# Token-major gates and outputs of three mixers with 512-column weight operands, the merged sum turned back, and the last norm spread over three engines

## What is computed

```python
def second_block(x, mem, ...):
    h = rmsnorm_2(x, norm_mix[l])
    (hq, hi, hff, hfb, hg, nq, nk, nv, cq, g_hg, g_na, g_ca) = split_cols(h @ w_in[l])
    y_hg = hgrn2_branch(hq, hi, hff, hfb, hg, lower_bounds[l], hg_gnorm[l], w_hg_o[l])
    y_na = neighbourhood_attention(nq, nk, nv, na_rpb[l], w_na_o[l])
    y_ca = memory_cross_attention(cq, mem_n, w_mem_kv[l], w_ca_o[l])
    merged = sigmoid(g_hg) * y_hg + sigmoid(g_na) * y_na + sigmoid(g_ca) * y_ca
    x = x + merged @ w_out[l]
    x = x + conv_ffn(rmsnorm_2(x, norm_ffn[l]), w_up[l], conv_w[l], conv_b[l], w_down[l])
    return rmsnorm_2(x, norm_final)
```

## Time and profile before

| | |
|---|---|
| median of 3 runs | 913.44 us (913.38 to 914.88) |
| profiled execution: its time | 913.59 us |
| profiled execution: span of the core | 911.7 us |
| mean granted clock of TensorE | 0.999 |
| PE / DVE / ACT / POOL busy | 99% / 71% / 55% / 34% |
| HBM read over the span | 179 GB/s |

### The profile page before, as it was taken

The page is one execution under the profiler, slowest core; times in us unless marked ns, Lnnn a source line. Parts: engine busy times, 40 slices in busy tenths (PEclk is TensorE's granted clock), DMA queues, the critical chain, the costliest instruction groups (busy, mean ns, idle before and its releaser), DMA issues.

```text
span 911.7 us, 16491 instructions
## 1 busy us (share of the span) xinstructions
PE 898.6 (99%) x6900; PEld 809.1 (89%) x6900; DVE 648.9 (71%) x804; ACT 505.5 (55%) x747; POOL 310.1 (34%) x117
## 2 busy tenths in 40 slices
PE   8999999999999999999999999999999999999997
PEld 7998986888888878999999989998999888888886
DVE  5986747888883257758798765857655689999623
ACT  7534747455554446755656565555545566666532
POOL 4000001666665410000000005846685166666542
PEclk9999999999999999999999999999999999999999
DMA  9693464555555544555545435443455365555551
GB/s 358 224 277 120 155 226 147 200 190 188 188 193 212 185 167 166 185 175 185 186 141 186 157 95 189 140 144 135 142 206 185 119 237 192 191 193 194 187 190 47
DMA packets 32299, 164.01 MB, mean 180 GB/s; under 512 B 9154, under 2 KB 11602, under 8 KB 13794
## 3 DMA queue, kind: packets, MB, share of 16 engines
q1 hardware_dynamic: 32162, 162.89, 52.0%
q0 software_dynamic: 64, 0.08, 0.0%
HBM read 161.40 MB, written 1.57 MB: 179 GB/s over the span
## 4 chain that ended last, share of the span: by engine, by line
PE 91%; DVE 4%; DMA 2%; ACT 2%; issue 1%; SPq 0%; DVEq 0%; ACTq 0%
PE ring L1699 31%; PE acc L1829 18%; PE ring L1733 9%; PE acc L1733 8%; PE ring L1780 6%; PE ring L1737 5%; PE acc L1737 4%; DMA raw<-wstream 2%; DVE w_lo L1116 1%; PE acc L1881 1%; PE acc L2038 1%; PE acc L1842 1%; PE acc L2134 1%; PE ring L1805 1%; PE ring L1718 1%
## 5 line engine op out<-in xcount | busy, mean ns | idle before, releaser
L642 POOL TENSOR_TENSOR w_lo<-raw,w_hi 128x1024 fp32r<-128x1024 f32 x101 | 289.9, 2872 | 579.1 <-ACT w_hi L690 579.0
L690 ACT CAST w_hi<-raw 128x1024 fp32r<-128x1024 f32 x284 | 297.1, 1052 | 312.3 <-PE ring L1699 124.5
L1116 DVE TENSOR_TENSOR w_lo<-raw,w_hi 128x1024 fp32r<-128x1024 f32 x183 | 229.1, 1263 | 119.1 <-ACT w_hi L690 109.7
L1699 PE MATMUL ring<-h,w_hi 128*128 128x256 f32 x1344 | 246.1, 285 | 2.0 <-issue 1.2
L1699 PEld LDWEIGHTS ring<-h,w_hi 128*128 128x128 f32 x1344 | 209.6, 192 | 3.7 <-issue 3.2
L1699 PE MATMUL ring<-h,w_lo 128*128 128x256 f32 x672 | 190.1, 283 | 0.0
L1699 PEld LDWEIGHTS ring<-h,w_lo 128*128 128x128 f32 x672 | 128.8, 192 | 1.3 <-issue 1.3
L1829 PE MATMUL acc<-w_hi,ff 128*128 128x512 f32 x340 | 91.1, 390 | 0.0
L1733 PE MATMUL ring<-h,w_hi 128*128 128x512 f32 x352 | 88.1, 392 | 0.0
L1733 PE MATMUL acc<-h,w_hi 128*128 128x512 f32 x336 | 84.6, 394 | 0.0
L1829 PEld LDWEIGHTS acc<-w_hi,ff 128*128 128x128 f32 x340 | 63.6, 188 | 13.2 <-DVE w_lo L1116 0.2
(11 more groups left out here) (283 smaller groups left out, 1286.6 us busy)
## 6 DMA issues: line engine op xcount, KB each, us to landing
raw<-wstream SPq DMA_DIRECT2D x142, 1024.0 KB, 4.9
u<-uconv SPq DMA_DIRECT2D x4, 426.0 KB, 9.9
toep_t<-toep SPq DMA_DIRECT2D x16, 96.0 KB, 3.1
x<-x_tok SPq DMA_DIRECT2D x2, 512.0 KB, 4.6
mem<-mem_tok SPq DMA_DIRECT2D x1, 1024.0 KB, 11.2
w_ple<-wproj SPq DMA_DIRECT2D x1, 1024.0 KB, 7.2
out_t<-y SPq DMA_DIRECT2D x4, 256.0 KB, 2.2
decay<-decay_tab SPq DMA_DIRECT2D x1, 768.0 KB, 6.5
```

Of the source, the lines that this page charges most:

```text
L642: nc.gpsimd.tensor_tensor(w_lo[:, u % UNITS], unit_of_raw(u), as_f32(w_hi[:, u % UNITS]), ALU.subtract).then_inc(lo_ready["pool"], 1)
L690: nc.scalar.copy(w_hi[:, u % UNITS], unit_of_raw(u)).then_inc(hi_ready, 1)
L1116: V.tensor_tensor(w_lo[:, u % UNITS], unit_of_raw(u), as_f32(w_hi[:, u % UNITS]), ALU.subtract).then_inc(lo_ready["dve"], 1)
L1699: last = mm(dst, w[a], src[:, b, kt], start=n == 0 and i == 0, stop=n == kts - 1 and i == 2)
```

## The change

It has three parts.

1. The 24 merge fills become 12 token-major ones: for each mixer and each half of the 1024 output features (512 columns) a gate fill (`ghg`, `gca`, `gna`, 32 blocks) and an output fill (`ohg` 32 blocks, `oca`, `ona` 16 blocks). A fill has two banks, one for each token half. The stationary tile is 128 tokens of `h` or of the mixer's output, the moving operand four weight blocks. The weights are laid out anew for this (`quarter_rows`). The stage has 20 slots of two units; `att_slot(s)` follows each. Products and sums are of 128x512.
2. `merged` is now token-major, so it is turned with `turn`, `turned_hi` and `turned_lo` ahead of `wout2`: turns 0 and 1 (features 0 to 511, both token halves) are issued by TensorE in the last slot but one, turns 2 and 3 between units 1 and 2 of the stream.
3. The end of the last norm: POOL multiplies the near half by the gain, DVE the far half; after the reciprocal DVE scales the near half and ACT the far half, and ACT stores its own.

The core of the diff:

```diff
-    ("cq", 0, 2, 16, "act"), ("mhg", 0, 8, 16, "dve"), ("mca", 0, 8, 12, "dve"), ("mna", 0, 8, 12, "dve"),
+    ("cq", 0, 2, 16, "act"), ("ghg", 0, 1, 32, "act"), ("ohg", 0, 1, 32, "dve"),
+    ("ghg", 1, 1, 32, "act"), ("ohg", 1, 1, 32, "dve"), ("gca", 0, 1, 32, "act"), ("oca", 0, 1, 16, "dve"),
+    ("gca", 1, 1, 32, "act"), ("oca", 1, 1, 16, "dve"), ("gna", 0, 1, 32, "act"), ("ona", 0, 1, 16, "dve"),
+    ("gna", 1, 1, 32, "act"), ("merged_x", 0, 2, 0, "dve"), ("ona", 1, 1, 16, "dve"), ("merged_x", 2, 2, 0, "dve"),
...
+ROW_BANKS = {"g": (0, 1), "o": (PJ - 1, PJ)}
+MERGED_BANKS = (PJ + 1, PJ + 2, 0, 1)
...
-_POOL_ONLY = [(INDEX[("mhg", 0)], INDEX[("mhg", 1)]),
-              (INDEX[("mca", 0)], INDEX[("mna", 7)])]
+_POOL_ONLY = [(INDEX[("ghg", 0)], INDEX[("ghg", 0)]),
+              (INDEX[("gca", 0)], INDEX[("ona", 1)])]
...
+        TURN_SLOT = MERGE_SLOTS - 2
...
             feed(NUNITS)
+            pool.wait_ge(load_gain["final"], 16)
+            pool.wait_ge(x_half, HALVED.index("down2") + 1)
+            pool.wait_ge(out_ready, 2)
+            nc.gpsimd.tensor_tensor(y_tok[:, 1, 0:512], x[:, 1, 0:512], gain["final"][:, 0:512], ALU.mult
+                                    ).then_inc(scaled_near, 1)
... (ACT)
+            for s in range(MERGE_SLOTS):
+                feed(slot_unit(s) + UNITS + 1)
+                act.wait_ge(pe_step, unit_step(slot_unit(s) + 1))
+                feed(slot_unit(s) + UNITS + 2)
+                if s == TURN_SLOT + 1:
+                    turned_hi("merged", 0)
+                    turned_hi("merged", 1)
+                name, j = ENDS_AT.get(s, ("", 0))
+                if name[:1] == "g":
+                    if s > 1:
+                        wait_read(act, *ENDS_AT[s - 2])
+                    for tt, src in enumerate(row_banks(name, j)):
+                        ins = A(row_gate[:, tt], src, ACT.Tanh, scale=0.5)
+                    ins.then_inc(freed["act"], 1)
+                att_slot(s)
+            turned_hi("merged", 2)
+            turned_hi("merged", 3)
             prime(ACT.Sqrt)
             feed(end_unit("wout2"))
...
+            act.wait_ge(scaled_far, 1)
+            act.wait_ge(out_ready, 3)
+            n = NORM["final", 1]
+            A(y_tok[:, 1, 512:], y_tok[:, 1, 512:], ACT.Identity, scale=sums[:, 2, n:n + 1]).then_inc(out_far, 1)
+            act.wait_ge(out_far, 1)
+            act.dma_start(out[:, 1, 512:], y_tok[:, 1, 512:]).then_inc(stored, 16)
... (DVE)
+            def merge_products(kind, j):
+                c = slice(512 * j, 512 * j + 512)
+                wait_read(dve, "g" + kind, j)
+                dve.wait_ge(pe_step, fill_step(fi("o" + kind, j)))
...
+                for tt, src in enumerate(row_banks("o" + kind, j)):
...
+                    ins = V.scalar_tensor_tensor(out=dst[:, tt, c], in0=row_gate[:, tt], scalar=1.0, in1=src,
+                                                 op0=ALU.add, op1=ALU.mult)
...
+                for tt in range(2):
...
+                    ins = V.tensor_tensor(merged[:, tt, c], merged[:, tt, c], q_tok[:, tt, c], ALU.add)
...
+            for s in range(MERGE_SLOTS):
+                if s < NHEADS:
+                    att_logits(s)
+                feed(slot_unit(s) + UNITS + 2)
+                if s == TURN_SLOT + 1:
+                    turned_lo("merged", 0)
+                    turned_lo("merged", 1)
+                name, j = ENDS_AT.get(s, ("", 0))
+                if name[:1] == "o":
+                    merge_products(name[1:], j)
+                if s < NHEADS:
+                    att_norm(s)
+                if 2 <= s < NHEADS + 2:
+                    att_lo(s - 2)
+            turned_lo("merged", 2)
+            turned_lo("merged", 3)
...
-            dve.wait_ge(x_half, HALVED.index("down2") + 1)
             near, far = slice(0, 512), slice(512, 1024)
-            scaled = link(V.tensor_tensor(y_tok[:, 1, near], x[:, 1, near], gain["final"][:, near], ALU.mult))
-            r = inverse("final", 1)
-            after(scaled)
-            V.tensor_scalar(y_tok[:, 1, near], y_tok[:, 1, near], r, None, ALU.mult).then_inc(out_ready, 1)
             dve.wait_ge(x_ready, 2 * SUMS.index("down2") + 2)
-            V.scalar_tensor_tensor(out=y_tok[:, 1, far], in0=x[:, 1, far], scalar=r, in1=gain["final"][:, far],
-                                   op0=ALU.mult, op1=ALU.mult).then_inc(out_ready, 1)
+            V.tensor_tensor(y_tok[:, 1, far], x[:, 1, far], gain["final"][:, far], ALU.mult).then_inc(scaled_far, 1)
+            n = NORM["final", 1]
+            dve.wait_ge(dev_ready, n + 1)
+            V.reciprocal(sums[:, 2, n:n + 1], sums[:, 1, n:n + 1]).then_inc(out_ready, 1)
+            dve.wait_ge(out_ready, 3)
+            dve.wait_ge(scaled_near, 1)
+            V.tensor_scalar(y_tok[:, 1, near], y_tok[:, 1, near], sums[:, 2, n:n + 1], None, ALU.mult
+                            ).then_inc(out_ready, 1)
... (TensorE)
+            def merge_rows(name, j, src, kts, ready=None):
+                banks = row_banks(name, j)
+                open_fill(name, j)
+                for kt in range(kts):
+                    u, c = at_block[0] // UB, 4 * (kt % 2)
+                    if c == 0:
+                        pe.wait_ge(lo_ready[LO_ENGINE[u]], lo_count(u, LO_ENGINE[u]))
...
+                    for tt in range(2):
+                        for part, w in ((0, w_hi), (0, w_lo), (1, w_hi)):
+                            last = mm(banks[tt], src[:, part, kt, tt * P:tt * P + P],
+                                      w[:, u % UNITS, c:c + 4].rearrange("p a b -> p (a b)"), ...)
...
+                    if kt % 4 == 3:
+                        s = (at_block[0] // UB - MERGE_UNIT) // 2 - 1
+                        if s == TURN_SLOT:
+                            turn("merged", 0, merged)
+                            turn("merged", 1, merged)
+                        att_slot(s)
...
+            def merged_kt(i, tt):
+                if i % 4 == 0:
+                    wait_turned("merged", 2 * (i // 4) + 1)
+
+            stream("wout2", lambda b, i, tt: merged_s[:, b, i, tt * P:tt * P + P], KT, merged_kt,
+                   ahead_of={2: ("merged", (2, 3))}, turned=merged)
```

More of the change, by code:

```diff
@@ L171 @@
 NORMED = ("first", "mem", "wout", "ple", "wout2")
-TURNS = ("first", "mem", "wout", "down", "ple", "wout2")
+TURNS = ("first", "mem", "wout", "down", "ple", "merged", "wout2")
 HALVED = ("wout2", "down2")
@@ L466, in wait_sum, with turned_part, row_banks @@
                 eng.wait_ge(pe_step, unit_step(end_unit(name) - 1))
+        def turned_part(name, k):
+            first, second = divmod(k, 2)
+            return (second, first) if name == "merged" else (first, second)
+        def row_banks(name, j):
+            return [flat(ring[:, b]) for b in filled_banks(fi(name, j))]
         def turned_h(name, k, part):
-            tt, q = divmod(k, 2)
-            return (mem_n if name == "mem" else h)[:, part, 4 * q:4 * q + 4, tt * P:tt * P + P]
+            tt, q = turned_part(name, k)
+            whole = {"mem": mem_n, "merged": merged_s}.get(name, h)
+            return whole[:, part, 4 * q:4 * q + 4, tt * P:tt * P + P]
         def turned_bank(name, k):
@@ L601, in _ @@
                 if n == FIRST_BLOCK[fi("wout2")] // 16:
-                    sp.wait_ge(pe_step, fill_step(fi("mca", 3)))
+                    sp.wait_ge(pe_step, fill_step(fi("oca")))
                     load_row("ffn2")
@@ L608, in _ @@
                     load_row("final")
-            for p in range(4):
+            for p in range(3):
                 tt, half = divmod(p, 2)
-                sp.wait_ge(out_ready, p + 1)
+                sp.wait_ge(out_ready, p + 1 if p < 2 else 4)
                 sp.dma_start(out[:, tt, 512 * half:512 * half + 512], y_tok[:, tt, 512 * half:512 * half + 512]
@@ new lines, in _ @@
+            pe.wait_ge(hg_root, 1)
+            for j in range(2):
+                merge_rows("ghg", j, h, KT)
+                merge_rows("ohg", j, o_hg_s, KT, lambda kt: pe.wait_ge(hg_split, kt // 2 + 1))
+            for j in range(2):
+                merge_rows("gca", j, h, KT)
+                pe.wait_ge(att_ready, 4)
+                merge_rows("oca", j, o_ca, 4)
+            for j in range(2):
+                merge_rows("gna", j, h, KT)
+                pe.wait_ge(att_ready, 8)
+                merge_rows("ona", j, o_na, 4)
@@ L2216, in token_blocks, with quarter_rows @@
                 for q in pairs]
+    def quarter_rows(w, first):
+        return [[w[kt * P:(kt + 1) * P, m * P:(m + 1) * P] for m in range(first, first + 4)] for kt in range(w.shape[0] // P)]
     def row_blocks(w, turn=0):
```

126 lines of the change are left out of this document (50 added, 76 removed).

## The result

| | median us | runs, us | ratio to before, 95% interval |
|---|---|---|---|
| before | 913.41 (6 runs) | 912.71 to 914.88 | |
| after | 918.38 (6 runs) | 917.16 to 920.09 | 1.0052 [1.0039, 1.0064] |

The changed kernel is 0.5% slower, and the interval stays clear of 1. Its profiled execution took 918.02 with a span of 916.1; the one of before 913.59 with 911.7. So the two executions differ by 4.4 us (their spans by 4.3), where the forecast's sum was +0.15.

A forecast was written before the change was run, and what follows sets the result against it. TensorE, busy 99% of the span, was taken as the bound. The terms -6.7 + 1.8 + 3.05 + 1.0 + 1.3 - 0.3 gave +0.15 us on the profiled execution, so 913.6 us was forecast, range 910.8 to 916.8.

The forecast's parts named there:

- 1, merge matmuls: Merge stage: 960 matmuls of 256 columns, 115.7 us, become 480 of 512 columns, 109.0 us; -6.7 us.
- 2, turns: Turning the merged sum back: sixteen 128x128 transposes added in two groups of eight; +1.8 us.
- 3, the wait: Ahead of the stream: TensorE waits for ACT's late copies of turns 0 and 1 and DVE's remainders; +3.05 us.
- 4, late weights: Stream's last units: casts and remainders of units 4 to 7 come late, DVE and POOL waiting for one another; +1.0 us.
- 5, attention: Attention work in the merge slots: shorter slots cover less softmax, mainly in slot 10; +1.3 us, range 0.4 to 3.3.
- 6, covered: Bank openings, the hg_root wait, tanh, SP's slots, POOL's units and ona 1's products stay hidden, at no cost.
- 7, the end: Last norm: work shared by POOL, DVE and ACT ends sooner; -0.3 us, from -0.5 to +0.5.
- rival (c): TensorE's clock falls in the 3 us wait; up to 5.4 us more at half the clock, 919; chance 0.05.
- signs of being wrong: Forecast wrong if the gap ahead of the stream is below 2 us or TensorE waits in more than two slots.
- slower side of 915.3: A measured time above 915.3 us counts as slower, taking in three rivals; chance 0.21.

The follow-up runs named there:

- e1: The changed kernel with ACT's copies and DVE's remainders of turns 0 and 1 ahead of the last merge slot's casts and wait: 913.36 us, ratio 0.9991 to before.
- e6: e5 with the stream's units 4 and 5 cast ahead of the copies of turns 2 and 3: 911.43 us, ratio 0.9971 to before.
- e9: e6 with DVE's two sums of each oca fill put a slot later, behind that slot's normalisation: 909.76 us, ratio 0.9960 to before.
- e5: e1 with DVE normalising the attention probabilities ahead of the merge's products and sums in each slot: 912.12 us, ratio 0.9981 to before.
- e14: The changed kernel run again, unchanged: 919.19 us, ratio 1.0050 to before.
- e4: The kernel before with its stream held until all eight features' parts of the merged sum are split: 921.23 us, ratio 1.0074 to before.
- e13: e9 run again, unchanged, on another chip than e6: 909.38 us, ratio 0.9945 to before.
- e3: The changed kernel with the old end of the last norm, DVE alone and all four stores by SP: 917.67 us, ratio 1.0043 to before.
- e8: The changed kernel with only DVE's attention normalisation moved ahead of the merge's products: 917.64 us, ratio 1.0035 to before.
- e15: e3 run again, the changed kernel with the old end of the last norm: 918.31 us, ratio 1.0045 to before.
- e11: The changed kernel with ACT's copies of turns 0 and 1 ahead of only the last slot's last cast: 916.61 us, ratio 1.0030 to before.
- e2: The changed kernel with 28 unused identity matmuls on TensorE in the wait ahead of the stream: 919.04 us, ratio 1.0058 to before.
- e7: The changed kernel with 12 unused identity matmuls on TensorE in the wait ahead of the stream: 917.32 us, ratio 1.0032 to before.
- e10: The kernel before with only the new end of the last norm put in: 914.81 us, ratio 1.0009 to before.

## Why the prediction was wrong

**1, merge matmuls.** Right for the matmuls, 0.5 too large for the difference. In steady stretches they are 0.2267 apart, where the forecast had 0.2271. What was off is the side before: its 0.1205 is a mean over 360 that also begins behind attention work, and from 660.11 to 690.11 before has 250 starts in 30.00 us, 0.1200 each, so 115.2 and not 115.7. The gain is 6.2 (115.2 less 480 x 0.2270 = 108.96) and not 6.7, or 13 ns per pair of 256 columns. The page's rule that spoke against the change (the Trainium skill, TensorE: Matmul & The Clock Gate, Back-to-back issue gap), a gain of 1.2 us, is not borne out by these rows. That section itself calls the spacing that of isolated matmuls and says that in a stream of weight loads and matmuls both set it; these rows have a weight load for each matmul, so the rule was not one to hold against the change.

**2, turns.** 0.87 and 0.79, 1.7 for 1.8.

**3, the wait.** Right: 3.07 for 3.05, and the order of its parts (the seven terms of the forecast, added again, give 3.07). It is the one number that e1 took away whole, together with what hung on it.

**4, late weights.** Right in size: 1.05 for 1.0. The conflict of DVE and POOL looks as forecast, though it came later by the 1.7 us of the low clock (a DVE remainder of 2.68 from 710.75, within POOL's two from 709.85). e6 shows that the wait on `w_lo` goes when the weights are fed first.

**5, attention.** +2.9 for +1.3, in the range of 0.4 to 3.3. Between the matmuls of the stage, the turn left out, are 24.9 us (134.74 - 0.87 - 108.96), against 22.0 before (137.24 - 115.2). Of this 2.1 are the two waits; the same view of before has none in the stage. The other 0.8 is mostly in the first matmuls behind each piece of attention work, which run slower than the steady spacing in both kernels and a little more so here; the forecast had no term for it. e9, with 0.3 us of waits left, still has 22.9. Of slot 10 I had put two outcomes, 0.4 and 2.7, and taken what I called the middle. The middle is 1.55, slot 1's 0.4 would come on top, so 1.3 does not follow from the working. The trace shows 1.8 in slot 10: DVE's product and sums first (640.93 to 643.40), then one `probs` multiply of 2.46 that lost to a POOL instruction. e5 and e9 show that it is the sums that matter, by where they stand.

**6, covered.** Held: the products of ona 1 (697.25 to 699.7) and POOL's units of the merge stage were on no chain.

**7, the end.** -0.1 by the ledger, nothing by the times, for -0.3: the mis-sized part is the store from ACT's queue, which no row had shown.

**The step that failed** is the weight of rival (c), the clock. The row that I held against it has TensorE busy for 4.79 of 5.60 us: it shows that the clock survives several stops that sum to 0.8 us, and says nothing of one of 3 us. The trace of before has only one wait of TensorE over 2 us, 2.4 ahead of its very first matmul, with no work before it to fall from. So nothing bore on the question, and with no row for it both ends, 0 and +5.4, belonged in the bounds of part 3. The chance of 0.05 was a choice, not a reading. The signs of being wrong could not catch it either: they asked for a wait below 2 us or waits in more than two slots, and the wait was 3.07 with waits in two slots; none asked for the granted clock behind the wait. The price was wrong too, in the other direction: 1.7 us, not up to 5.4. That is 1.7 / 0.2271, some 8 matmuls at half the clock; the window from 702 has full clock again.

The terms on the executions' spans, measured: -6.24 + 1.66 (turns) + 3.07 + 1.05 + 2.87 - 0.07 (all behind the stream) + 1.73 (clock) = +4.07, and 0.27 from ahead of the stage, 4.3. Of the miss of 4.2 us against +0.15 the clock is 1.7, attention 1.6, the matmuls 0.5, the end 0.2 and the start 0.3 (less 0.1 for the turns). Without the low clock the profiled execution would still have been 2.7 us over that of before, 916.3: inside the range given, but on the slower side of 915.3. So two steps failed: the attention term, mis-sized by more than its own size, carried the result off the forecast's middle, and the clock, left out of the sum, took it out of the range.

(The Trainium skill, TensorE: Matmul & The Clock Gate, What's actually happening, has the clock drop to 1.2 GHz when the engine idles; the runs agree, behind waits of 1.8 to 4.9 us, at a price of 1.6 us (e14, slot 10: 1.36 + 6.90 for 1.01 + 5.68) to 2.2 us (e4).)

## What to carry to other kernels

- A wait on the engine that bounds the kernel costs more than its length: add the low clock behind it (here 1.7 us for a wait of 3.1, 2.2 for one of 4.9, and some executions already fell behind 1.8) unless rows of the same kernel show waits of that length with the clock kept, in more than one execution.
- Where a result is turned on TensorE, the copies out of the banks belong in the copying engine's list at the place where the turn is issued, ahead of any wait for later matmuls; a slot of cover written in one engine's list is worth nothing if another engine's list undoes it.
- Between two outcomes of a race, forecast one of them. And keep DVE operations with two SBUF operands out of the chain to the next matmul while POOL has instructions in a row: putting them a slot later was worth 1.0 to 2.4 us (the ratios of e9 and e13 against e6's, of which only e13's is clear of e6's interval).

## What the runs showed of the hardware

- TensorE's granted clock fell from the 2.4 to the 1.2 GHz level behind a single wait of 3.1 us in every profiled execution that had it and left it empty (after, e3, e8, e14, e15: the next 24 matmuls took 7.02 to 7.34 us, 5.44 in e1), behind 4.9 us during the wait itself (e4), behind 2.1 us in the profiled one and by the mean clocks not in two of twelve (e11). Behind the 1.8 us of attention slot 10 it fell in the profiled executions of e1, e2, e7 and e14 and not in those of after, e3, e11 and e15.
- Whether such a wait makes a kernel's times spread more is not shown: e11's twelve runs lie within 4.6 us and e13's six within 0.7, but e10's twelve, without such a wait, lie within 4.1.
- Matmuls of 512 columns, each with its own weight load, were 0.2267 us apart in steady stretches of both loops, of 256 columns 0.1200; the first ones behind attention work were up to 0.34 apart (660.50 to 660.84).
- Two DVE sums of 128x512 between SBUF tiles took 5.28 us beside two POOL instructions in a row and 1.29 without them.
- A store of 256 KB landed 2.4 us after its issue from ACT's queue (2.5 in e10), one store in each of twelve executions; those from SP's queue took 2.1 or 2.2 in the median.
